# Delta rule of a hybrid decoder step: products of the inverse's first level by alternating halves, VectorE's copies for level two moved ahead, and a fill issued by two queues

## What is computed

```python
kb = kc * bc[..., None]
lmat = jnp.where(strict, jnp.einsum('nbhid,nbhjd->nbhij', kb, kc) * decay, 0.0)
tmat = lax.linalg.triangular_solve(eye + lmat, eye, left_side=True, lower=True, unit_diagonal=True)
u = jnp.einsum('nbhij,nbhjd->nbhid', tmat, vc * bc[..., None])
w = jnp.einsum('nbhij,nbhjd->nbhid', tmat, kb * jnp.exp(gc)[..., None])

def step(S, xs):
    v_new = u_i - jnp.einsum('bhcd,bhde->bhce', w_i, S)
    att = jnp.einsum('bhid,bhjd->bhij', q_i, k_i) * dec_i
    o = (q_i * exp(g_i)) @ S + att @ v_new
    S = S * exp(g_last) + (k_i * exp(g_last - g_i)).T @ v_new
```

## Time and profile before

| what | value |
|---|---|
| median of 3 runs | 3161.38 us (3157.72 to 3161.7) |
| the profiled execution: its time, its span | 3158.1 us, 3156.4 us |
| TensorE busy over the span | 2939.9 us (93%) |
| VectorE, ScalarE, GpSimd busy | 1579.7, 1204.3, 771.7 us |
| mean granted clock of TensorE | 0.963 |
| stage E in the trace | about 2317 to 2870 us |

### The profile page before, as it was taken

One profiled execution on the slowest core, in us unless ns is written; L12 is line 12 of the kernel. 1 busy time (PEld: TensorE's weight loads), 2 busy tenths in 40 slices (PEclk: granted clock), 3 DMA queues, 4 the chain that ended last, 5 costly groups with the idle time before them and its releaser, 6 DMA issues. The chain is left out here.

```text
span 3156.4 us, 56373 instructions
## 1 busy us (share of the span) xinstructions
PE 2939.9 (93%) x21172; PEld 2540.3 (80%) x21172; DVE 1579.7 (50%) x2503; ACT 1204.3 (38%) x2960; POOL 771.7 (24%) x1153
## 2 busy tenths in 40 slices
PE   7999999979999989999699999999958999997999
PEld 5777899968888867755599999998948888885767
DVE  4653124148888954321355555541135776664251
ACT  5421111159999944422312121212125556552000
POOL 2331000036666632221000000000035555541020
PEclk9999999989999989999799999999978999998999
DMA  4443111172440157798512121222134446445243
GB/s 129 122 139 122 47 35 48 62 189 74 102 98 16 44 181 236 251 339 284 177 62 81 61 81 61 73 68 73 54 113 119 124 128 148 124 107 171 81 128 122
DMA packets 403609, 368.80 MB, mean 117 GB/s; under 512 B 84140, under 2 KB 327793, under 8 KB 398213
## 3 DMA queue, kind: packets, MB, share of 16 engines
q1 hardware_dynamic: 389689, 330.16, 35.2%
q0 software_dynamic: 10240, 33.56, 3.2%
q10 hardware_dynamic: 3440, 1.88, 0.3%
HBM read 250.86 MB, written 114.84 MB: 116 GB/s over the span
## 5 line engine op out<-in xcount | busy, mean ns | idle before, releaser
L1867 PE MATMUL D_ps_y<-D_xT_hi,D_w_hi 128*128 128x416 f32 x1280 | 453.1, 354 | 9.6 <-DVE D_xT_lo L2072 9.6
L1868 PE MATMUL D_ps_y<-D_xT_lo,D_w_hi 128*128 128x416 f32 x1280 | 449.1, 351 | 0.0
L1869 PE MATMUL D_ps_y<-D_xT_hi,D_w_lo 128*128 128x416 f32 x1280 | 448.6, 350 | 0.0
L1041 DVE TENSOR_TENSOR_SCAN B_left<-B_ps_z,B_left,B_one 128x512 f32<-128x512 f32 (+3 forms) x272 | 289.8, 1111 | 19.1 <-ACT B_ps_z L1002 16.7
L1089 POOL TENSOR_TENSOR B_a<-B_take,B_left 128x512 f32<-128x512 f32 (+3 forms) x272 | 255.7, 958 | 140.9 <-PE B_ps_a L954 82.1
L1867 PEld LDWEIGHTS D_ps_y<-D_xT_hi,D_w_hi 128*128 128x128 f32 x1280 | 240.5, 188 | 12.3 <-issue 9.7
L1869 PEld LDWEIGHTS D_ps_y<-D_xT_hi,D_w_lo 128*128 128x128 f32 x1280 | 240.7, 188 | 3.2
L1868 PEld LDWEIGHTS D_ps_y<-D_xT_lo,D_w_hi 128*128 128x128 f32 x1280 | 241.2, 188 | 2.0
L1000 ACT ACTIVATE B_take<-B_ps_z,B_bias 128x512 f32<-128x512 f32 (+3 forms) x320 | 208.6, 652 | 25.5 <-PE B_ps_z L944 18.5
L939 PE MATMUL B_ps_z<-B_qk 128*128 128x128 f32 (+3 forms) x928 | 191.8, 338 | 21.1 <-DVE B_bias L1027 20.2
L1002 ACT ACTIVATE B_ps_z<-B_ps_z,B_bias 128x512 f32<-128x512 f32 (+3 forms) x320 | 200.9, 628 | 0.0
(11 more groups left out here) (447 smaller groups left out, 6678.3 us busy)
## 6 DMA issues: line engine op xcount, KB each, us to landing
scratch_strips<-D_out SPq DMA_DIRECT2D x32, 1040.0 KB, 4.7
scratch_turned<-A_turned SPq DMA_DIRECT2D x64, 256.0 KB, 2.9
D_w_raw<-in_w_in_odd SPq DMA_DIRECT2D x32, 512.0 KB, 5.9
B_qk<-scratch_turned SPq DMA_DIRECT2D x30, 384.0 KB, 10.9
scratch_mixT<-A_gate SPq DMA_DIRECT2D x8, 1040.0 KB, 3.9
D_xT_lo<-scratch_xT SPq DMA_DIRECT2D x5, 1664.0 KB, 15.3
A_x<-in_x_prompt SPq DMA_DIRECT2D x16, 512.0 KB, 3.8
C_pg_held<-in_cache_k SPq DMA_DIRECT2D x32, 256.0 KB, 3.3
```

The source lines that it names most:

```text
L1041: dve.tensor_tensor_scan(buf[:, hh, at:at + w][:, ::-1], p_z[n % Z][:, 0:w][:, ::-1], one[:, 0:1].to_broadcast([P, w]), buf[:, hh, at + w: ...
L1867: pe.matmul(dst, w_hi[:, slot, k, :], xT_hi[:, k, cols], start=(k == 0), stop=False)
L1868: pe.matmul(dst, w_hi[:, slot, k, :], xT_lo[:, k, cols], start=False, stop=False)
L1869: mm = pe.matmul(dst, w_lo[:, slot, k, :], xT_hi[:, k, cols], start=False, stop=(k == KC - 1))
```

## The change

- `block_x` and `block_y` take the four heads outside and the two halves inside, so that neighbouring products belong to different halves. Both halves' waits now stand in front of all products.
- On VectorE `quarter_g` moves in front of `on` and part 0; part 1 of the solution moves to where part 2 was, behind `half_g`, and part 2 to the slot's end.
- `grow_l` has four buffers and four semaphores instead of two.
- SP issues the loads of tiles 6 and 7 in slot -5, ahead of the first gather, instead of in slots -4 and -3.
- Of the first gather's eight stores and the first scatter's eight loads, SP issues four and ScalarE the other four.

```diff
-        grow_l, grow_a = (sb(n, [P, 2, U, P]) for n in ("grow_l", "grow_a"))
+        grow_l, grow_a = sb("grow_l", [P, 4, U, P]), sb("grow_a", [P, 2, U, P])
...
+        def blocks_out(eng, s, which):
+            at = SW * s % LR
+            for b in which:
+                rows = slice(b * BK, (b + 1) * BK)
+                eng.dma_start(io["blocks"][rows, :, :].rearrange("u i j -> i u j"),
+                              ln[rows, at:at + SW, :, rows].rearrange("p w u j -> p (w u) j")).then_inc(s_mo, 16)
+
+        def solved_in(eng, s, which):
+            for b in which:
...
@@ SP, load_a
-                if w >= 2:
-                    sp.wait_ge(s_el, w - 1)
-                grow(grow_l[:, w % 2, :, :], w, s_gl[w % 2])
+                if w >= 4:
+                    sp.wait_ge(s_el, w - 3)
+                grow(grow_l[:, w % 4, :, :], w, s_gl[w % 4])
@@ SP, gather and scatter
+                blocks_out(sp, s, range(NB // 2 if s == 0 else NB))
...
+                solved_in(sp, s, range(NB // 2 if s == 0 else NB))
@@ SP, slots
-                if real(w + LA + 2) and w + LA + 2 > 1:
+                if real(w + LA + 2) and w + LA + 2 > 1 and w not in (-4, -3):
                     load_a(w + LA + 2)
+                if w == SW - 1 - LA:
+                    load_a(w + LA + 3)
+                    load_a(w + LA + 4)
@@ TensorE
             def block_x(w):
-                for hf in range(2):
-                    if hf == 0:
-                        pe.wait_ge(s_sc[w // SW % 2], 16 * NB * (w // SW // 2 + 1))
-                        pe.wait_ge(s_nm, w + 1)
-                    if w > 0:
-                        pe.wait_ge(s_ut[hf], (5, 3)[hf] * w)
-                    r = rows(hf)
-                    for u in range(U):
+                pe.wait_ge(s_sc[w // SW % 2], 16 * NB * (w // SW // 2 + 1))
+                pe.wait_ge(s_nm, w + 1)
+                if w > 0:
+                    pe.wait_ge(s_ut[0], 5 * w)
+                    pe.wait_ge(s_ut[1], 3 * w)
+                for u in range(U):
+                    for hf in range(2):
+                        r = rows(hf)
                         mm = pe.matmul(p_l[hf][r, u * HF:(u + 1) * HF], nm[r, w % 2, u, r],
                                        ut0[r, w // SW % 2, w % SW * U + u, 0, :], start=True, stop=True)
-                    mm.then_inc(s_x[hf], 1)
+                        if u == U - 1:
+                            mm.then_inc(s_x[hf], 1)
             def block_y(w):
                 for hf in range(2):
                     pe.wait_ge(s_gm[hf], (3, 2)[hf] * w + 1)
-                    r = rows(hf)
-                    for u in range(U):
+                for u in range(U):
+                    for hf in range(2):
+                        r = rows(hf)
                         pe.matmul(p_l[hf][r, u * HF:(u + 1) * HF], ut0[r, w // SW % 2, w % SW * U + u, 1, :], gm[r, u, :],
                                   start=True, stop=True)
...
@@ ScalarE, slots, behind decay_l(a)
+                    if a == SW - 1:
+                        act.wait_ge(s_ln, SW)
+                        blocks_out(act, 0, range(NB // 2, NB))
+                    if a == SW + 2:
+                        act.wait_ge(s_to, 16)
+                        act.wait_ge(s_zero, 2)
+                        solved_in(act, 0, range(NB // 2, NB))
@@ VectorE
-                    if w == -3 and n == 2:
+                    if w == -3 and n == 1:
...
+                if real(lv_w):
+                    quarter_g(lv_w)
                 if real(w - 1):
                     dve.wait_ge(s_co, w)
...
                     by_column(on[:, :, :], p_o, fo[:, w - 1, :], s_on)
                 solve_part(w, 0)
-                if real(lv_w):
-                    quarter_g(lv_w)
-                solve_part(w, 1)
...
                     half_g(lv_w)
-                solve_part(w, 2)
+                solve_part(w, 1)
...
                     dve.tensor_tensor(qe[:, b % 2, :, :], q[:, b % 2, :, :], erow[:, :, :], ALU.mult).then_inc(s_qe, 1)
+                solve_part(w, 2)
```

More of the change, by code:

```diff
@@ L2191, in stage_e @@
         s_z = [sem(f"z_in{i}") for i in range(2)]
-        s_gl = [sem(f"grow_l_in{i}") for i in range(2)]
+        s_gl = [sem(f"grow_l_in{i}") for i in range(4)]
         s_ga = [sem(f"grow_a_in{i}") for i in range(2)]
@@ L2237, in stage_e @@
                  (g_o[:, :], io["o_norm"].rearrange("o e -> e o"))]
+        def blocks_out(eng, s, which):
[6 more added lines that the diff above has]
+            for b in which:
+                rows = slice(b * BK, (b + 1) * BK)
+                at = slice(b * BK % HF, b * BK % HF + BK)
+                eng.dma_start(ut0[rows, s % 2, :, :, at].rearrange("p u a j -> p (u a) j"),
+                              io["solved"][rows, :, :, :].rearrange("u a i j -> i (u a) j")).then_inc(s_sc[s % 2], 16)
         @block.sync
@@ L2404, in block_y @@
                     pe.wait_ge(s_gm[hf], (3, 2)[hf] * w + 1)
-                    r = rows(hf)
-                    for u in range(U):
+                for u in range(U):
+                    for hf in range(2):
+                        r = rows(hf)
                         pe.matmul(p_l[hf][r, u * HF:(u + 1) * HF], ut0[r, w // SW % 2, w % SW * U + u, 1, :], gm[r, u, :],
                                   start=True, stop=True)
-                    for u in range(U):
+                for u in range(U):
+                    for hf in range(2):
+                        r = rows(hf)
                         mm = pe.matmul(p_l[hf][r, (U + u) * HF:(U + u + 1) * HF], gm[r, u, :],
                                        ut0[r, w // SW % 2, w % SW * U + u, 1, :], start=True, stop=True)
-                    mm.then_inc(s_y[hf], 1)
+                        if u == U - 1:
+                            mm.then_inc(s_y[hf], 1)
             def quarter_x(w):
@@ L2677, in exponent_l @@
             def exponent_l(w):
-                dve.wait_ge(s_gl[w % 2], 16 * (w // 2 + 1))
+                dve.wait_ge(s_gl[w % 4], 16 * (w // 4 + 1))
                 if w > 1:
                     dve.wait_ge(s_dl, w - 1)
-                dve.tensor_tensor(e_l[:, w % 2, :, :], grow_l[:, w % 2, :, :], mask_l[:, :, :], ALU.add).then_inc(s_el, 1)
+                dve.tensor_tensor(e_l[:, w % 2, :, :], grow_l[:, w % 4, :, :], mask_l[:, :, :], ALU.add).then_inc(s_el, 1)
             def by_column(dst, src, column, s):
@@ L2773, in exponent_l @@
             def exponent_l(w):
-                pool.wait_ge(s_gl[w % 2], 16 * (w // 2 + 1))
+                pool.wait_ge(s_gl[w % 4], 16 * (w // 4 + 1))
                 pool.wait_ge(s_el, w)
                 pool.wait_ge(s_dl, w - 1)
-                pool.tensor_tensor(e_l[:, w % 2, :, :], grow_l[:, w % 2, :, :], mask_l[:, :, :], ALU.add).then_inc(s_el, 1)
+                pool.tensor_tensor(e_l[:, w % 2, :, :], grow_l[:, w % 4, :, :], mask_l[:, :, :], ALU.add).then_inc(s_el, 1)
             def exponent_a(w):
```

## The result

The changed kernel takes 3134.28 us in the median (3128.5 to 3136.0, 4 runs), the kernel before, on the same chip, 3160.12 us (3157.72 to 3161.7, 4 runs). The ratio is 0.9916, interval [0.9898, 0.9933]: 25.8 us faster by the medians. The forecast was 3124 with a range from 3104 to 3150, a gain of 34.8. The profiled execution took 3132.84 us, 25.3 less than the one before.

What follows compares the result with a forecast made beforehand. Stage E's slots were held to lose 37 us to disturbances, mainly TensorE's 31.0 us of waits for `quarter_g`. Gains of 27.8 (23 slots), 4.5, 1.0 and 1.5 made 34.8 us: 3123.3, stated as 3124, range 3104 to 3150.

Steps and rivals of the forecast that it cites:

- The mechanism: VectorE's `quarter_g` copies, moved in front of `on` and the solution, end TensorE's 31.0 us of waits and their lower clock.
- Products in alternating halves: Alternating `block_x` and `block_y` run a pair in the time of one: slot 13.62 us, 0.58 gained.
- the first product of level two 1.08 later: In each slot `v_new` starts at 2.80 us, and level two's first product 1.08 us after it.
- Rival 2: The halves of `block_x` and `block_y` don't overlap, the changed order does nothing: 26 us less, 3150; chance 0.06.
- The late `block_g`: VectorE's solution work at the slot's end delays the next `block_g` by 2.2 us, in six slots, w = 2 to 22.
- The meeting with `e_a`: Two steps of the solution's part 1 on VectorE are slowed beside GpSimd's `e_l` and `e_a`: about 1.0 us more.
- The clock behind it: After the long wait at `block_y` in six slots, TensorE's lower clock costs 1.5 us more each; bounds 0 and 3.
- Rival 1: Each new wait at `block_y` keeps the lower clock for a whole slot: slower, 3187 us; chance 0.07.
- Slots 23 to 30: The last slots, with little of either cover or stall left, gain 1.5 us.
- Slot -1: The low-clock slot before the loop saves half of `block_x` and `block_y`, as far as ScalarE's copies follow: 1.0 us.
- The fill: Before the loop, earlier `grow_l` loads gain 2.5 us, two queues at the scatter 2.0; together 4.5, bounds 2 and 7.8.
- Rival 3: New transfer waits, four us late in five slots, give back 20: 3144; chance 0.18, shared with more lateness at `block_y`.

## Why the prediction was right, and where its sizes were off

The mechanism and the sign held: the wait for `quarter_g` went, from 31.0 to 4.9 us, and the order on VectorE is by itself the largest part (17.4 us). The gain was 25.8 where 34.8 was forecast. By terms, in the profiled execution:

**Products in alternating halves: 0.58 us a slot forecast, 0.16 measured.** This is the term that was mis-sized. `block_x`, `block_y` and `v_new` came as worked out (`v_new` 2.90 against 2.80). The step that failed is "the first product of level two 1.08 later": it took `v_new` alone to stand in front of `quarter_x`, and left out ScalarE's four copies. Of the 0.16, 0.09 are there with VectorE's order alone (14.11), so alternation gave 0.07. Over 23 slots this is 23 x (14.04 - 13.62) = 9.7 us short, and the result without the solution confirms that alternation as such is worth nothing. Rival 2's 3150 asked for halves that don't overlap; they do, and the slot gains hardly more.

**The late `block_g`: 6 x 2.2 forecast.** In slots w = 2, 6, 10, 14, 18 and 22 `block_y` starts 3.7, 1.8, 2.1, 1.8, 1.3 and 1.8 us later than in an undisturbed slot, 12.4 in all against 13.2: 8.7 in the last five, 1.7 each, and the total is near the forecast only by the 3.7 of w = 2. The meeting with `e_a` came as said, once and not twice: a step of 0.94 us in part 1 (profile above), where the next longer one took 0.48. The 3.7 of w = 2 hold another such meeting, of `t_out`'s copy, 0.38 otherwise, with GpSimd's `nm`; one line each of VectorE and GpSimd:

```profile
2409.00 1.45 DVE L2664 COPY E_t_out<-E_t_out 128x256 f32<-128x256 f32 x1
```

```profile
2408.95 1.26 POOL L2850 TENSOR_TENSOR E_nm<-E_ln,E_level 128x512 f32<-128x512 f32 x1
```

The copy ends 0.24 us behind `nm`. It has one input, so of the two conditions that the Trainium skill names for the lock in "SBUF — State Buffer", section "SBUF: two separate sides", two inputs in SBUF or a mode that takes both ports, it would be the second. That it was held is what the trace shows.

**The clock behind it: 6 x 1.5 forecast.** Of the five slots from w = 6 to 22 one lost 1.1 us and four nothing; w = 2 lost 1.8. That is 2.9 instead of 9.0. Rival 1, the lower level for a whole slot, did not happen here, but nearly so in other kernels (19.87 above). Its reason, that slot -1 stood at 0.57 because its products came with gaps, was not tried.

**Not foreseen:** slot 0 takes 11.79, 2.25 less than the others, and slots 1, 5, 17 and 21 together 3.3 more. So the 23 slots gained 27.8 - 9.7 + 0.8 + 6.1 - 1.0 = 24.0, as measured.

That the clock gave back 6.1 of the 9.7 is luck. The change without alternation has the loop of the kernel with VectorE's order alone but for the two further buffers of `grow_l`. With the order alone the five late slots from w = 6 to 22 have waits of 1.39 to 1.76 us, one of them fell to the lower clock, and the 23 slots took 345.67 us (window above). In the change without alternation the five waits are 1.41 to 1.76 us, all five slots fell, and the 23 took 354.45:

```profile
2376.53:2730.98 354.45, 338.15 (x4020) 306.50 (x4020) 252.86 (x700) 215.98 (x965) 208.73 (x386) 0.93 0.54 136
```

So the loop of one order of work differed by 9 us between two profiles, mostly by how often the clock fell.

**Slots 23 to 30: 1.5 forecast, 0 for 23 to 29.** Slots 23 and 24 gained 4.2 us with the wait for `quarter_g`. But the forecast counted six late `block_g` and there is a seventh, at w = 26: a wait of 2.73 us and a slot of 15.95 instead of 13.13. Slot 25 lost 0.7 as well. The other slots without keys take 13.15 instead of 12.93, since there `block_y`, which waits for both halves now, starts at 1.74 instead of 1.18, and the copies behind it are late by more than it saves.

**Slot -1: 1.0 forecast, 0.5 measured.**

**The fill: 4.5 forecast, 4.0 measured,** by other shares than the 2.5 and 2.0. The stage itself began 0.5 us earlier (2316.86 instead of 2317.36), which isn't the change's. From there the solution is stored 2.8 us earlier, by the mechanism forecast: the wait of 5.76 us for `grow_l` is gone, and VectorE waits once for ScalarE, which first issues its four stores (`kt`, in the fill):

```profile
2339.03 0.69 DVE L2705 TENSOR_TENSOR E_kt<-E_ps_a,gd 128x512 f32<-128x512 f32 x1 [3.12 <-ACT E_junk_k L2552]
```

The scatter gained only 0.7, from 7.69 between the store's issue (2359.74) and the first product to 6.97. The forecast took the gain for what two queues save in issuing, but the first product waits for the last of the eight loads to land. Why they land 0.40 us apart wasn't tried.

From the last start of `block_x` to the span's end are 317.3 us after and 314.0 before. In the other executions here, which have the same work there, these are 314.1 to 316.4, so most of the 3.3 us is what this stretch varies by from one execution to another.

Rival 3, transfers, did not come with the change, but was next in line: it came as soon as the solution ended later.

**Open:** whether alternation is worth the 3.5 us by which the medians with and without it differ. By the profiles of slots w = 6 to 22 a spell of the lower clock at `block_y` cost 1.2 to 4.3 us (mean 3.1, nine slots of three kernels) with `block_y` by halves, and 1.1 to 2.7 (mean 1.6, six slots of two kernels) with alternation, against the same slot's sum without it. Three such spells would make some 4 us, but their number goes from one to five of five slots on either side, and this was only argued.

## What to carry to other kernels

When products of two halves are made to run beside each other, look at who empties both results: if one engine does it in sequence, the end of its queue sets the next product, and starting that queue early by finishing one half first can be worth as much as the faster products. An engine's idle time in a slot is of use only on the right side of the work it is late with; here 1.45 us in front of `quarter_g` stood beside a lateness of 2 us behind it. And in a loop with a tight transfer chain, work moved to a later place on one engine can show up as another engine's wait, several steps away: here VectorE's later steps made a load late, the load GpSimd, and GpSimd VectorE and TensorE.

## What the runs showed of the hardware that was not expected

After waits of nearly the same length TensorE's clock went either way: 1.40 us, then a slot at 0.74; 1.76 us, in the same kernel and at the same place of the slot, then 1.00; 2.58 us, 1.00. The first two each followed an undisturbed slot (14.11 and 14.12 us) and had the same instructions. What decides stays open.
